# Order of two loops in the score matmuls of a gated scan: blocks outside, heads inside

## The chip, the cores and the metric

The kernel runs on one core of a Trainium2 chip. Its time is that of one execution on the device, in microseconds (us). The engines of the core run side by side and wait for each other through semaphores: TensorE (PE in the profile; its weight loads are PEld), VectorE (DVE), ScalarE (ACT), GpSimd (POOL) and SyncE (SP), which issues DMAs.

## The reference, cut to what matters

The model is one block with a recurrence and dilated attention, then two layers of a hybrid block. In each hybrid layer one branch is a gated linear scan with 4 heads of 64 channels, run forwards (`d` = 0) and backwards (`d` = 1):

```
S_t = diag(f_t) S_{t-1} + k_t v_t^T        o_t = S_t^T q_t
# in chunks; inside a chunk, with a = cumsum(log f):
scores[t, s] = sum_c q[t, c] * k[s, c] * exp(a[t, c] - a[s, c])     for s <= t
out[t] = sum_s scores[t, s] v[s]  +  (q[t] * exp(a[t])) @ state
```

The sum over the 64 channels `c` of one head is the contraction of the score matmuls that this document is about. Sequence: 2048 positions and 256 of context, all in float32.

## The kernel before, in words

`stage_hgrn_scan` (L1339) is called four times: two layers by two directions. It holds the channels on the partitions: a pair `pr` of heads fills 128 partitions, head `h` = 0 on partitions 0 to 63 and head `h` = 1 on 64 to 127. The positions are cut in blocks of 128, and a step of the scan takes `n` blocks: the first step has n = 2 (the context), the four after it n = 4.

The products of gates within a block are built up in levels. A step has LV = 8 levels `lv`, and each level has two parts, one for each pair `pr`. One such part, (lv, pr), is called a group here; a step has 16 of them. In a group

- TensorE computes for each of the two heads and each of the n blocks a 128x128 score matrix over 64 partitions (L1419): stationary operand `kb`, moving operand `qT` at level 0 and `qf` later. The output of head h goes into PSUM bank `pS[pr][h]` (`ps_s` in the profile), one 128-column piece for each block. A float32 matmul shows as two weight loads and two matmuls in the profile, so a group of n = 4 has 16 records of each, one of n = 2 has 8. The last matmul of the group raises `sc`.
- After it TensorE issues one of the eight k-slices of the projection of the next step (L1393, tile `ps_f`, two records over 128 partitions and 512 columns). In the last step of a scan there is no next one, and no such matmul.
- VectorE waits for `sc`, multiplies the gates of this level into `qf` (L1528) and `kb` (L1530), makes the products for the next level (L1532, shorter at each level; it raises `up`), and copies the two banks under the mask of the level into `scores_t` (L1541, twice; at level 0 there is only L1537, twice). The copies raise `cp`.

A group (lv, pr) on TensorE waits for `up` and `cp` of (lv - 1, pr): the operands must be updated, and the banks read. The two pairs take turns, so that VectorE works on one while TensorE works on the other.

After the levels come the transposes of `kb` (L1428), the state matmuls (L1433) and, block by block, the output matmuls (L1445 and L1453, whose operands are 64 columns wide, two heads in turn). VectorE starts the next step with L1512 to L1514, which wait for the last output matmul.

All orders are written out by hand in the loops of each engine; there is no planner. The instructions of TensorE are issued in program order.

Of the kernel before, what the change touches and what calls it, by code (L numbers as in the profile page):

```python
# [13 lines left out]
P = 128  # L14
# [12 lines left out]
HD = 64  # L27
# [1311 lines left out]
def stage_hgrn_scan(env, layer, d, hT, qT, vN, oT, out_ctx):  # L1339
# [17 lines left out]
    with ExitStack() as ctx:  # L1357
# [22 lines left out]
        @block.sync  # L1380
        def _(sp):
            env.load_groups(sp, g + 1 + 1)

        @block.tensor
        def _(pe):
            w = env.group_here(pe, g)

            def project(s, pr, k):
                col, n = steps[s]
                if k == 0 and s >= 1:  # L1390

                    pe.wait_ge(fk.h, fk.at(4 * (s - 1) + 2 * pr + 2))
                mm = pe.matmul(pf[pr][:, 0:n * P], w[:, k, pr * P:(pr + 1) * P], hT[:, k, col:col + n * P],  # L1393
                               start=(k == 0), stop=(k == KT - 1))
                if k == KT - 1:
                    mm.then_inc(pj.h, 1)

            for pr in range(2):
                for k in range(KT):
                    project(0, pr, k)  # L1400
            for s, (col, n) in enumerate(steps):
                for lv in range(LV):
                    for pr in range(2):
                        if lv < 2:
                            pe.wait_ge(qi.h, qi.at(4 * s + 2 * pr + 2))
                        else:
                            pe.wait_ge(up.h, up.at(14 * s + 2 * (lv - 2) + pr + 1))

                        if lv >= 1:
                            pe.wait_ge(cp.h, cp.at(2 * (NU * s + 2 * (lv - 1) + pr) + 2))  # L1410
                        elif s >= 1:
                            pe.wait_ge(su.h, su.at(sum(2 * m for _, m in steps[:s])))
                            pe.wait_ge(tc.h, tc.at(2 * s))
                        for h in range(2):
                            lo = HD * h
                            for i in range(n):
                                cs = slice(i * P, (i + 1) * P)
                                rhs = qT[lo:lo + HD, pr, col + i * P:col + (i + 1) * P] if lv == 0 else qf[lo:lo + HD, pr, cs]
                                mm = pe.matmul(pS[pr][h][:, cs], kb[lo:lo + HD, pr, cs], rhs, start=True, stop=True)  # L1419
                        mm.then_inc(sc.h, 1)  # L1420
                        if s + 1 < NSTEP:
                            project(s + 1, pr, lv)
                for pr in range(2):

                    pe.wait_ge(up.h, up.at(14 * s + 12 + pr + 1))
                    pe.wait_ge(cp.h, cp.at(2 * (NU * s + 2 * (LV - 1) + pr) + 2))
                    for i in range(n):
                        mm = pe.transpose(pS[pr][0][:, i * P:(i + 1) * P], kb[:, pr, i * P:(i + 1) * P], env.ident[:, :])  # L1428
                    mm.then_inc(tm.h, 1)
                for pr in range(2):  # L1430
                    pe.wait_ge(tc.h, tc.at(2 * s + pr + 1))
                    for i in range(n):
                        mm = pe.matmul(pS[pr][1][:, i * P:(i + 1) * P], kbn[:, pr, i * P:(i + 1) * P],  # L1433
                                       vN[:, col // P + i, pr * P:(pr + 1) * P], start=True, stop=True)
                    mm.then_inc(um.h, 1)
                order = range(n - 1, -1, -1) if d else range(n)
                for x, i in enumerate(order):
                    n_done = sum(m for _, m in steps[:s]) + x
                    for pr in range(2):
                        cs = slice(i * P, (i + 1) * P)  # L1440

                        if x == 0 and s >= 1:
                            pe.wait_ge(oc.h, oc.at(2 * (s - 1) + pr + 1))
                        for h in range(2):
                            pe.matmul(pO[pr][HD * h:HD * (h + 1), cs],  # L1445
                                      vN[:, col // P + i, pr * P + h * HD:pr * P + (h + 1) * HD],
                                      sT[:, pr, h, cs], start=True, stop=False)

                        if n_done >= 1:
                            pe.wait_ge(su.h, su.at(2 * (n_done - 1) + pr + 1))  # L1450
                        for h in range(2):
                            lo = slice(HD * h, HD * (h + 1))
                            mm = pe.matmul(pO[pr][lo, cs], st[lo, pr, n_done % 2, lo], qf[lo, pr, cs],  # L1453
                                           start=False, stop=True)
                        mm.then_inc(om.h, 1)
            pe.wait_ge(om.h, om.at(2 * WT))
            pe.sem_inc(env.sem("w_used").h, 1)

        @block.scalar
        def _(act):  # L1460
            def sigmoids(s):
                n = steps[s][1]
                for pr in range(2):
                    act.wait_ge(pj.h, pj.at(2 * s + pr + 1))
                    if s >= 1:

                        act.wait_ge(qi.h, qi.at(4 * (s - 1) + 4))
                    act.activation(fn[:, pr, 0:n * P], pf[pr][:, 0:n * P], ACT.Sigmoid).then_inc(fk.h, 1)
                    act.activation(kn[:, pr, 0:n * P], pf[pr][:, 0:n * P], ACT.Sigmoid, scale=-1.0).then_inc(fk.h, 1)

            sigmoids(0)
            for s, (col, n) in enumerate(steps):
                if s + 1 < NSTEP:
                    sigmoids(s + 1)
                for pr in range(2):
                    act.wait_ge(tm.h, tm.at(2 * s + pr + 1))
                    if s >= 1:
                        act.wait_ge(um.h, um.at(2 * (s - 1) + pr + 1))
                    act.activation(kbn[:, pr, 0:n * P], pS[pr][0][:, 0:n * P], ACT.Copy).then_inc(tc.h, 1)
                if d == 0:  # L1480
                    for pr in range(2):
                        act.wait_ge(om.h, om.at(2 * sum(m for _, m in steps[:s + 1])))
                        act.activation(oT[:, pr, col:col + n * P], pO[pr][:, 0:n * P], ACT.Copy).then_inc(oc.h, 1)
# [13 lines left out]
        def _(dve):  # L1497
# [6 lines left out]
            for s, (col, n) in enumerate(steps):  # L1504
                w = n * P
                ready, done = (fl, 4) if layer == 1 else (fk, 4)
                for pr in range(2):
                    dve.wait_ge(ready.h, ready.at(4 * s + 2 * pr + 2))
                    if s >= 1:
                        dve.wait_ge(tm.h, tm.at(2 * (s - 1) + pr + 1))  # L1510
                        dve.wait_ge(om.h, om.at(2 * sum(m for _, m in steps[:s])))
                    dve.tensor_copy(f[:, pr, 0:w], fn[:, pr, 0:w])  # L1512
                    dve.tensor_copy(kb[:, pr, 0:w], kn[:, pr, 0:w]).then_inc(qi.h, 1)
                    dve.tensor_tensor(qf[:, pr, 0:w], qT[:, pr, col:col + w], fn[:, pr, 0:w], ALU.mult).then_inc(qi.h, 1)  # L1514
# [29 lines left out]
                for x, i in enumerate(order):  # L1544
                    n_done = sum(m for _, m in steps[:s]) + x
                    for pr in range(2):
                        if x == 0:
                            dve.wait_ge(um.h, um.at(2 * s + pr + 1))
                            dve.wait_ge(up.h, up.at(14 * s + 12 + pr + 1))
                        if n_done >= 1:  # L1550

                            dve.wait_ge(om.h, om.at(2 * (n_done - 1) + pr + 1))
                            dve.wait_ge(su.h, su.at(2 * (n_done - 1) + pr + 1))
                        for h in range(2):
                            lo = slice(HD * h, HD * (h + 1))
                            ins = dve.scalar_tensor_tensor(
                                out=st[lo, pr, (n_done + 1) % 2, HD * h:HD * (h + 1)],
                                in0=st[lo, pr, n_done % 2, HD * h:HD * (h + 1)],
                                scalar=pp[lo, pr, poff[7] + i:poff[7] + i + 1],
                                in1=pS[pr][1][lo, i * P + HD * h:i * P + HD * (h + 1)], op0=ALU.mult, op1=ALU.add)  # L1560
                        ins.then_inc(su.h, 1)
# [1110 lines left out]
```

## Time and profile before

| | |
|---|---|
| median of 3 runs | 6555.46 us (6535.63 to 6560.89) |
| span of the profiled execution | 6529.7 us, 77413 instructions |
| the profiled execution's own time | recorded as its span alone |
| mean granted TensorE clock | 0.910 of full speed |
| TensorE matmul, busy | 5885.4 us, 90% |
| TensorE weight loads, busy | 4344.2 us, 67% |
| VectorE, busy | 2844.0 us, 44% |
| ScalarE, busy | 1763.7 us, 27% |

The span runs from the first to the last instruction. Busy is the share of it in which at least one instruction of the engine was under way. The two scans of the first hybrid layer lie between 2116 and 2680 us, those of the second between 4503 and 5040 us. The clock is granted at one of two levels, 0.5 (1.2 GHz) or 1.0 (2.4 GHz).

### The profile page before, as it was taken

Reading aid. Unit: us, or ns where it says so; the run is one execution under the profiler, and the core shown is the slowest. Engines: PE = TensorE matmul, PEld = TensorE weight load, DVE = VectorE, ACT = ScalarE, POOL = GpSimd, SP = SyncE. Lnnn points to the kernel's source line nnn. Section 1 sums busy time; section 2 is a strip of 40 time slices with the busy share of each in tenths; the row PEclk is TensorE's granted clock in tenths of the full one; section 3 lists DMA queues with packets and bytes.
Section 4 is the critical chain, followed back from the end, with each engine's and each line's share of the span. In section 5 each row is a group of like instructions: output and inputs, shape, how many; then the busy total and the mean of one; then the engine's idle time right before and its main releaser. Section 6 shows DMA issues by size and latency. Waiting matters only on the chain. (4 is left out here: it accounts for less than half of the span.)

```text
span 6529.7 us, 77413 instructions
## 1 busy us (share of the span) xinstructions
PE 5885.4 (90%) x30276; PEld 4344.2 (67%) x30276; DVE 2844.0 (44%) x6558; ACT 1763.7 (27%) x4082; POOL 328.0 (5%) x381
## 2 busy tenths in 40 slices
PE   5879998989969999799999988969998899999889
PEld 2338887765548666567777466867666667775667
DVE  2220124433334666625555035345667535551254
ACT  2221015431134000114444123042000134442231
POOL 0000110000010000210000000000000300000000
PEclk8989998857779978799999999989898999999999
DMA  4001110134320000000000111220000000001212
GB/s 158 13 13 50 35 60 28 55 131 136 130 87 20 1 7 1 11 14 1 1 1 1 47 49 49 97 87 14 1 7 1 20 4 1 1 1 33 63 49 94
DMA packets 145404, 256.78 MB, mean 39 GB/s; under 512 B 10796, under 2 KB 89748, under 8 KB 144276
## 3 DMA queue, kind: packets, MB, share of 16 engines
q1 hardware_dynamic: 107700, 211.98, 9.3%
q10 hardware_dynamic: 37344, 39.85, 1.8%
q8 instruction: 244, 4.00, 0.3%
q14 instruction: 116, 0.95, 0.0%
HBM read 195.81 MB, written 55.98 MB: 39 GB/s over the span
## 5 line engine op out<-in xcount | busy, mean ns | idle before, releaser
L1903 PEld LDWEIGHTS ps_pv<-y_t,probs_t 128*128 128x128 f32 x4640 | 588.6, 192 | 153.3 <-issue 142.9
L1980 DVE TENSOR_REDUCE soft<-ps_scores 128x1 f32<-128x512 f32 (+1 forms) x648 | 410.3, 633 | 495.8 <-PE ps_scores L1866 494.7
L1903 PE MATMUL ps_pv<-y_t,probs_t 128*128 128x64 f32 x4640 | 579.7, 270 | 31.4 <-DVE y_t L2018 30.8
L1419 PEld LDWEIGHTS ps_s<-qf,kb 64*128 64x128 f32 x4032 | 423.1, 214 | 194.5 <-DVE products L1532 127.0
L1419 PE MATMUL ps_s<-qf,kb 64*128 64x128 f32 x4032 | 472.8, 315 | 8.6 <-DVE scores_t L1541 8.5
L1277 DVE TENSOR_TENSOR features_low<-h_t,features_high 128x1024 fp32r<-128x1024 f32 x260 | 304.0, 1171 | 354.6 <-ACT features_high L1242 354.1
L644 PE MATMUL ps_proj<-weight_ring,h_t 128*128 128x256 f32 x2048 | 448.5, 381 | 2.7 <-PE ps_proj L644 2.2
L644 PEld LDWEIGHTS ps_proj<-weight_ring,h_t 128*128 128x128 f32 x2048 | 388.9, 191 | 57.6 <-issue 5.4
L1959 ACT ACTIVATE probs<-ps_scores,soft 128x512 f32<-128x512 f32 (+1 forms) x648 | 407.6, 642 | 16.6 <-DVE soft L1989 16.6
L1214 PE MATMUL ps_proj<-features_high,weights_high 128*128 128x512 f32 (+1 forms) x880 | 346.2, 393 | 60.1 <-DVE features_low L1277 30.8
L1945 ACT ACTIVATE probs_t<-ps_pt 128x512 f32<-128x512 f32 (+1 forms) x392 | 205.0, 523 | 686.3 <-PE ps_pt L1883 676.2
L1883 PE MATMUL ps_pt<-ident,probs 128*128 128x128 f32 x2320 | 370.9, 278 | 7.7 <-ACT probs L1959 7.5
L1242 ACT ACTIVATE features_high<-h_t 128x1024 fp32r<-128x1024 f32 x260 | 259.7, 1001 | 420.9 <-PE ps_proj L1214 359.0
L1393 PE MATMUL ps_f<-h_t,weight_ring 128*128 128x512 f32 (+1 forms) x640 | 341.7, 633 | 5.3 <-PEq L1357 2.9
L1541 DVE COPY_PREDICATED scores_t<-level_masks,ps_s 128x512 f32<-128x512 uint8 (+1 forms) x560 | 340.3, 660 | 0.0
L1214 PE MATMUL ps_proj<-features_high,weights_low 128*128 128x512 f32 (+1 forms) x880 | 340.2, 387 | 0.0
L1214 PE MATMUL ps_proj<-features_low,weights_high 128*128 128x512 f32 (+1 forms) x880 | 339.9, 386 | 0.0
L1883 PEld LDWEIGHTS ps_pt<-ident,probs 128*128 128x128 f32 x2320 | 275.3, 150 | 76.3 <-issue 66.4
L1866 PE MATMUL ps_scores<-y_t 128*128 128x512 f32 (+1 forms) x648 | 292.2, 550 | 1.7 <-PEq L1647 1.7
L1866 PE MATMUL ps_scores<-k_second,y_t 128*128 128x512 f32 (+1 forms) x648 | 293.5, 551 | 0.0
L1693 PE MATMUL ps_proj<-weight_ring,h_t 128*128 128x256 f32 x1120 | 256.8, 385 | 27.6 <-PEq L1580 27.6
L1693 PEld LDWEIGHTS ps_proj<-weight_ring,h_t 128*128 128x128 f32 x1120 | 211.5, 193 | 59.1 <-issue 29.8
(308 smaller groups left out, 9159.0 us busy)
## 6 DMA issues: line engine op xcount, KB each, us to landing
weight_ring<-in_w_in_dram SPq DMA_DIRECT2D x40, 1024.0 KB, 6.4
mod_weights<-in_w_mod_dram ACTq DMA_DIRECT2D x24, 1024.0 KB, 5.2
x_rows<-h_rows SPq DMA_DIRECT2D x32, 512.0 KB, 5.9
t_rows<-t_rows SPq DMA_DIRECT2D x64, 256.0 KB, 2.6
x_res<-h_rows SPq DMA_DIRECT2D x32, 512.0 KB, 3.5
res<-result SPq DMA_DIRECT2D x48, 264.0 KB, 2.0
res_rows<-res SPq DMA_DIRECT2D x48, 264.0 KB, 3.9
h_t<-v_rows SPq DMA_DIRECT2D x3, 4096.0 KB, 13.8
```

The source lines that it names most:

```text
L644: mm = pe.matmul(ps[u % 4][:, 0:GC], hT[:, k, t * P:(t + 1) * P], w[:, k, :], start=(k == 0), stop=(k == KT - 1))
L1214: mm = pe.matmul(bank[:, 0:n], w_[:, k0 + k, i * P:(i + 1) * P], f_[:, k, 0:n], start=start, stop=stop)
L1277: dve.tensor_tensor(self.fl[:, s % NB, :, 0:n], self.hT[:, k0:k0 + KS, c0:c0 + n], self.fh[:, s % NB, :, 0:n].bitcast(F32), ALU.subtract). ...
L1393: mm = pe.matmul(pf[pr][:, 0:n * P], w[:, k, pr * P:(pr + 1) * P], hT[:, k, col:col + n * P], start=(k == 0), stop=(k == KT - 1))
L1419: mm = pe.matmul(pS[pr][h][:, cs], kb[lo:lo + HD, pr, cs], rhs, start=True, stop=True)
L1541: dve.copy_predicated(dst, env.levmask[:, 8 * d + l, None, :].to_broadcast([P, n, P]), src)\
L1693: mm = pe.matmul(ps[u % 4][:, 0:GC], hT[:, k, t * P:(t + 1) * P], w[:, k, :], start=(k == 0), stop=(k == KT - 1))
L1866: pe.matmul(ps[c][:, 0:n * P], QT[:, i, t * P:(t + 1) * P], keys[kv][:, (k0 + 4 * c) * P:(k0 + 4 * c + n) * P], start=True, stop=True).the ...
L1883: mm = pe.transpose(pt[c % 2][:, j * P:(j + 1) * P], pr[:, before(u, c) % NPR, j * P:(j + 1) * P], env.ident[:, :])
L1903: mm = pe.matmul(pv[:, 0:HD], pT[:, before(u, c) % 4, j * P:(j + 1) * P], VN[:, k0 + k, kv * HD:(kv + 1) * HD], start=(k == 0), stop=(k == ...
L1959: act.activation(pr[:, i % NPR, 0:n * P], ps[c][:, 0:n * P], ACT.Exp, bias=st[:, b, 0, NC + 1:NC + 2], scale=HD ** -0.5, accum_out=st[:, b ...
L1980: dve.tensor_reduce(st[:, u % 2, 0, c:c + 1], ps[c][:, 0:tiles(u, c) * P], AXX, ALU.max).then_inc(mx.h, 1)
```

## The change

In the group's matmuls the loop over the n blocks becomes the outer one and the loop over the two heads the inner one. The same 2n matmuls are issued with the same operands into the same places of PSUM, and the last one is in both orders that of head 1 and the last block; it raises `sc` as before. No wait, no semaphore, and no other engine's code changes.

```
-                        for h in range(2):
-                            lo = HD * h
-                            for i in range(n):
-                                cs = slice(i * P, (i + 1) * P)
+                        for i in range(n):
+                            cs = slice(i * P, (i + 1) * P)
+                            for h in range(2):
+                                lo = HD * h
                                 rhs = qT[lo:lo + HD, pr, col + i * P:col + (i + 1) * P] if lv == 0 else qf[lo:lo + HD, pr, cs]
                                 mm = pe.matmul(pS[pr][h][:, cs], kb[lo:lo + HD, pr, cs], rhs, start=True, stop=True)
                         mm.then_inc(sc.h, 1)
```

Before, the order for n = 4 is head 0 with blocks 0, 1, 2, 3 and then head 1 with blocks 0, 1, 2, 3. After, it is block 0 with heads 0, 1, then block 1 with heads 0, 1, and so on.

## Rows read from the trace of the kernel before

**Rows 1.** The page: busy time of TensorE, and its granted clock in 40 slices.
```profile
PE 5885.4 (90%) x30276; PEld 4344.2 (67%) x30276; DVE 2844.0 (44%) x6558; ACT 1763.7 (27%) x4082; POOL 328.0 (5%) x381
...
PEclk8989998857779978799999999989898999999999
```

**Rows 2.** Instructions of tile ps_s: count, duration min/median/max in ns, first and last start.
```profile
L1419 PEld LDWEIGHTS ps_s<-qf,kb x4032: 182/188/336, 2119.6 to 5028.2; 64*128 64x128 f32 x192
L1419 PE MATMUL ps_s<-qf,kb x4032: 271/272/580, 2119.6 to 5028.4; 64*128 64x128 f32 x192
L1419 PEld LDWEIGHTS ps_s<-y_t,kb x576: 182/330/335, 2116.2 to 4993.7; 64*128 64x128 f32 x192
...
L1433 PEld LDWEIGHTS ps_s<-y_t,kb_rows x288: 186/192/337, 2145.1 to 5034.8; 128*128 128x128 f32 x144
```

**Rows 3.** Windows over levels of the twelve n = 4 steps with projection: us, busy, clock.
```profile
2150.73:2193.85 43.12, 43.12 (x289) 29.29 (x290) 32.77 (x76) 1.09 (x2) 0.00 (x0) 1.00 0.00 1
...
2425.53:2486.10 60.57, 60.56 (x289) 40.04 (x290) 32.72 (x76) 1.09 (x2) 0.00 (x0) 0.69 0.00 1
...
sum 581.89, PE 581.87 PEld 393.51 DVE 393.14 ACT 13.02 POOL 8.40; mean PE 48.49 PEld 32.79 DVE 32.76 ACT 1.09 POOL 0.70
```

**Rows 4.** Timeline of one group and the next, n = 4, clock 1.0: start, duration.
```profile
2221.66 1.52 PEld L1419 LDWEIGHTS ps_s<-qf,kb 64*128 64x128 f32 x16 [0.76 <-issue]
2221.66 1.71 PE L1419 MATMUL ps_s<-qf,kb 64*128 64x128 f32 x16
...
2223.30 1.12 PE L1393 MATMUL ps_f<-h_t,weight_ring 128*128 128x512 f32 x2
2223.41 0.43 DVE L1528 TENSOR_TENSOR qf<-qf,products 128x256 f32<-128x256 f32 x1 [0.49 <-PE ps_s L1419]
...
2224.29 1.33 DVE L1541 COPY_PREDICATED scores_t<-level_masks,ps_s 128x512 f32<-128x512 uint8 x2
...
2224.36 1.71 PE L1419 MATMUL ps_s<-qf,kb 64*128 64x128 f32 x16
```

**Rows 5.** Timeline of one group of an n = 2 step, clock 1.0.
```profile
2121.35 0.53 PEld L1419 LDWEIGHTS ps_s<-qf,kb 64*128 64x128 f32 x8 [0.76 <-issue]
2121.35 0.72 PE L1419 MATMUL ps_s<-qf,kb 64*128 64x128 f32 x8
2122.00 0.30 PEld L1393 LDWEIGHTS ps_f<-h_t,weight_ring 128*128 128x128 f32 x2
```

**Rows 6.** Timeline of the state matmuls, 128 partitions, clock 1.0.
```profile
2253.04 1.86 PEld L1433 LDWEIGHTS ps_s<-y_t,kb_rows 128*128 128x128 f32 x16
2253.05 2.04 PE L1433 MATMUL ps_s<-y_t,kb_rows 128*128 128x128 f32 x16
```

**Rows 7.** Timeline of the output matmuls, which take the two heads in turn, clock 1.0.
```profile
2255.39 0.44 PE L1453 MATMUL ps_o<-qf,state 64*64 64x128 f32 x4
2255.76 0.20 PEld L1445 LDWEIGHTS ps_o<-scores_t,y_t 128*64 128x64 f32 x4 [0.17 <-issue]
```

**Rows 8.** Timeline of two groups, n = 4, clock 0.5.
```profile
2272.20 3.09 PE L1419 MATMUL ps_s<-qf,kb 64*128 64x128 f32 x16
...
2277.23 3.09 PE L1419 MATMUL ps_s<-qf,kb 64*128 64x128 f32 x16
```

**Rows 9.** Windows over the levels of the four last steps, without projection.
```profile
2327.99:2369.55 41.56, 40.20 (x257) 39.10 (x257) 31.45 (x72) 0.00 (x0) 0.00 (x0) 0.54 0.00 1
...
4713.77:4750.72 36.95, 33.57 (x257) 31.58 (x257) 30.95 (x73) 0.00 (x0) 0.00 (x0) 0.72 0.00 1
...
sum 157.26, PE 148.42 PEld 142.81 DVE 125.20 ACT 0.00 POOL 0.00; mean PE 37.11 PEld 35.70 DVE 31.30 ACT 0.00 POOL 0.00
```

**Rows 10.** Timeline in a last step, clock 1.0.
```profile
2348.80 0.42 DVE L1528 TENSOR_TENSOR qf<-qf,products 128x256 f32<-128x256 f32 x1
...
2349.06 1.68 PE L1419 MATMUL ps_s<-qf,kb 64*128 64x128 f32 x16 [0.35 <-DVE scores_t L1541]
...
2350.82 0.42 DVE L1528 TENSOR_TENSOR qf<-qf,products 128x256 f32<-128x256 f32 x1
```

## The prediction, made before the changed kernel ran

> **What bounds the kernel now.** I began with the page. TensorE is busy 90% of the span and its clock is at full speed for most of it [rows 1], so a shorter stretch of matmuls is worth its time, provided that TensorE is what ends last just there. The instructions of the tile `ps_s` [rows 2] give 4032 + 576 = 4608 matmul records at L1419: 4 scans of one n = 2 step (16 groups of 8) and four n = 4 steps (64 groups of 16).
>
> Then the windows over the levels of each step. There are two kinds of n = 4 step. In twelve steps with the projection beside the scores TensorE is busy 581.87 of 581.89 us, VectorE 32.76 us of 48.49 in the mean [rows 3]: TensorE is the bound. The same rows show the clock: 43.12 us a step at 1.0, up to 60.57 at 0.69. In the four last steps TensorE and VectorE hand over to each other: 157.26 us, of which VectorE is busy 125.20 [rows 9].
>
> The timeline of one group [rows 4] gives the period: 2224.36 - 2221.66 = 2.70 us, of which the scores take 1.64 until the projection starts (2223.30) and the projection 1.06. VectorE has 0.49 us of idle time in a period, waiting for the score matmuls. 16 periods make the 43.12 us.
>
> **What a group's 16 records cost now.** The state matmuls use all 128 partitions, so their loads come one after another: 16 loads in 1.86 us, the last of them 0.19 long, so 15 pitches of (1.86 - 0.19)/15 = 0.111 us [rows 2, 6]. Measure the score groups with that pitch. With n = 4 the 16 loads take 1.52 us: (1.52 - 0.19)/0.111 = 12 pitches, not 15 [rows 4]. With n = 2 the 8 loads take 0.53 us: 3 pitches, where one after another would be 7 [rows 5]. So with n = 2 the two heads, 4 loads each, run wholly side by side, and with n = 4 only 3 of 8 do. My reading: TensorE looks a short way ahead in the program, some 8 instructions (4 pairs of load and matmul). With n = 2, head 0 has 4 pairs, and head 1 is in sight at once. With n = 4, head 0 has 8 pairs, and head 1 comes in sight when the fifth has been issued; it starts 5 pitches late, overlaps for three, and ends alone.
>
> The Trainium skill ("TensorEngine Tiling (Array Packing)", Key Properties) says that different tiles can load weights and multiply in parallel, and that a change of the tiling mode drains the engine. Rows 5 agree with the first, and the second touches nothing here, since both heads use 64x128 tiles.
>
> **The change, part by part.**
> 1. The order. With heads in turn, four pairs of look-ahead always hold both heads: they start together, as with n = 2. The loads then need 7 pitches in place of 12, so a group is shorter by 5. Counted the other way: the n = 2 group takes 0.65 us until the projection starts [rows 5]; four more pairs for each head, side by side, add 4 x 0.111 = 0.44, together 1.10 against 1.64. The saving is 0.54 us a group at clock 1.0, and the period becomes 2.70 - 0.54 = 2.15.
> 2. Whether VectorE lets it. Its work in a step is at most 32.77 us [rows 3]; 16 periods of 2.15 are 34.5. It is covered by 1.7 us a step, and no more: were the score matmuls free, the step could still not fall below about 32. In a period with little product work VectorE's own pitch is 2350.82 - 2348.80 = 2.02 us [rows 10]. The chain of one pair (scores 1.15 to their end, VectorE some 2.2, handing over some 0.2: 3.6) fits into two periods (4.3). So TensorE stays the bound, barely, and the projection and its copies keep their place.
> 3. At clock 0.5 the group takes 3.09 us [rows 8], the period is 2277.23 - 2272.20 = 5.03, and 5 pitches of twice the length save 1.07: 3.96. Both clocks give a period shorter by about a fifth. If the clock rises after the same time as before, the groups that fall into the slow time are more, and a step saves what one at full speed does: 16 x 0.54 = 8.67 us (with the unrounded 0.542). If it rises after as many groups as before, 20% of 581.89 = 116. I take the first: 12 x 8.67 = 104 us.
> 4. The last steps. There is no projection to hide VectorE, and the sum changes kind. Below is VectorE's busy time, 31.3 us a step [rows 9], plus its wait for the first group, 1.2 to 2.1: 32.5 to 33.4. Above is the handing over at clock 0.5: scores 3.09 - 1.07 = 2.0, VectorE 2.1 to 2.2, two signals, 4.4 us a level, 7 of them and a shorter first of 3.5: 34.3. I take 33.5: 157.26 - 4 x 33.5 = 23 us saved. The ends are 130 and 137.2 for the four, so 20 to 27 saved.
> 5. The n = 2 steps: the heads already run side by side [rows 5]. Nothing.
> 6. Everything else (transposes, state, output matmuls, copies, DMAs) keeps its instructions and its waits. A step ends earlier, and so the next starts earlier; the weights for the next stage are loaded during the scan and their landing is far from its end. Nothing.
>
> Sum: 104 + 23 = 127 us. The profiled execution has a span of 6529.7, and would have 6402. The median of the runs is 25.8 us over that span; I carry this over, as something that the change doesn't touch: 6555.5 - 127.4 = **6428 us**.
>
> **The unknown: the clock.** The rows show that a busy TensorE isn't enough to raise it at once: in the step of 2425.53 it was 0.69 in the mean with TensorE busy 60.56 of 60.57 us [rows 3]. All twelve steps together lose 581.9 - 12 x 43.12 = 64 us to the lower clock. If denser matmuls bring it back sooner, up to some 25 us of it are won. If it goes the other way, see the fourth rival.
>
> **Rivals.**
> - *The supply of instructions is the limit.* Side by side, TensorE needs two pairs, 4 instructions, in 0.111 us, 28 ns each. The fastest long stretch that the trace shows is that of the output matmuls, 8 records in 2255.76 - 2255.39 = 0.37 us, 46 ns each [rows 7], though there the change between tile shapes sets the pace. With the first 8 instructions in sight and 24 more at 46 ns, the last starts at 1.10 us, and the group takes 1.31: 0.21 lost of 0.54, 192 groups, 40 us: 6468. For it: no row shows 28 ns over more than the half of a group. Against it: the n = 2 group's 16 instructions come at this rate [rows 5], and 36 instructions in a period of 2.15 are 60 ns in the mean. Chance 0.10.
> - *The change doesn't do what it says*: both orders overlap alike, or the look-ahead isn't what sets head 1 back, but a limit on side-by-side work after a few pairs. Time 6555. Against it is the pair of 3 pitches for 8 loads and 12 for 16. Chance 0.07. The Trainium skill ("TensorE: Matmul & The Clock Gate", the table at its top) gives TensorE a queue of 64 with a partial reorder window. If that window were 64 instructions long, the 32 of a group would fit, head 1 would start with head 0 already today, and the change would be worth nothing. By that rule this rival is the forecast; rows 4, where 16 loads take 12 pitches and not 7, speak against it.
> - *The overlap of today is lost*: with a switch of tile at every matmul the pairs go strictly one after another, 15 pitches in place of 12. A group costs 3 x 0.111 = 0.33 more, 256 groups: 85 us, time 6640. It decides from 12 pitches on. Against it: head by head in turn is what the output matmuls do, and 4 of their records take 0.44 us, 0.27 of it the last matmul's own [rows 2, 7]. Chance 0.04.
> - *The clock falls in the steps with projection*, because TensorE's work is done in less time and VectorE begins to end last; in the last steps, where TensorE has idle time of 0.35 us in a group, the clock is 0.54 to 0.72 [rows 9, 10]. With all twelve steps at 0.5: 12 x 16 x 3.96 = 760 us against 581.9, less 23: 155 us more, 6711. It breaks even where a step with projection takes 50.4 us. Against it: with a period of 2.15 TensorE has no idle time. Chance 0.04.
> - The forecast: 0.75, for the arithmetic rests on two measured groups.
>
> **Range and chances.** The forecast's own range is 6390 to 6455: clock won (25) and runs that differ by 25 us among themselves. For 8 in 10 I add the first rival and leave out the rest: 6385 to 6480. About 0.5%, 33 us, is what a measurement of this kernel can tell from none. Forecast and first rival are faster by more: 0.85. Same 0.07, slower 0.08.
>
> **What the profile of the changed kernel would show.** The n = 4 group: 16 loads in about 0.97 us, 16 matmuls in 1.15, the projection 1.10 after the group's start; the period 2.15 at clock 1.0 and 3.96 at 0.5. VectorE idle before L1528 under 0.1 us in place of 0.49. A step with projection at full clock 34.5 us, a last step 33 to 34. The n = 2 group unchanged at 0.72. I am wrong if the group takes 1.3 us or more, if VectorE's groups take more than 2.15 us in a row so that TensorE waits for `scores_t` in steps with projection, or if the clock in the steps differs.

## The result, and the profile after

| | before | after |
|---|---|---|
| median of 4 runs | 6545.55 us (6517.28 to 6560.89) | 6343.07 us (6334.53 to 6353.71) |
| span of the profiled execution | 6529.7 us | 6351.9 us |
| mean granted TensorE clock | 0.910 | 0.92 |

The ratio is 0.969, with a 95% interval of 0.9662 to 0.9718. The kernel is faster by some 200 us. I had forecast 6428 us and a range from 6385 to 6480: the sign is right, the time is below the range.

The timeline of the changed kernel shows one n = 4 group and what follows, at full clock; the columns are start, duration, engine, line and tile, as in [rows 4]:

```profile
2182.70 0.97 PEld L1419 LDWEIGHTS ps_s<-qf,kb 64*128 64x128 f32 x16 [0.76 <-DVE products L1532]
2182.70 1.16 PE L1419 MATMUL ps_s<-qf,kb 64*128 64x128 f32 x16
2183.80 0.30 PEld L1393 LDWEIGHTS ps_f<-h_t,weight_ring 128*128 128x128 f32 x2
2183.80 1.12 PE L1393 MATMUL ps_f<-h_t,weight_ring 128*128 128x512 f32 x2
2183.91 0.42 DVE L1528 TENSOR_TENSOR qf<-qf,products 128x256 f32<-128x256 f32 x1
...
2184.85 1.16 PE L1419 MATMUL ps_s<-qf,kb 64*128 64x128 f32 x16
```

The 16 loads take 0.97 us in place of 1.52, so 7 pitches of 0.111 us in place of 12. The projection starts 1.10 us after the group, and the period is 2184.85 - 2182.70 = 2.15 us. VectorE's L1528 has no idle time before it, where it had 0.49. All of this is as forecast. What isn't shows in the windows. First the twelve steps with projection (length, busy time and count of PE, PEld, DVE, ACT, POOL, then the clock), to be read against [rows 3]:

```profile
2167.67:2202.03 34.36, 34.36 (x289) 20.52 (x290) 32.30 (x76) 1.08 (x2) 0.00 (x0) 1.00 0.00 1
...
2392.17:2428.11 35.94, 35.94 (x289) 21.25 (x290) 32.30 (x76) 1.08 (x2) 0.00 (x0) 0.95 0.00 1
...
4676.53:4713.81 37.28, 37.28 (x289) 22.49 (x290) 32.27 (x76) 1.09 (x2) 0.85 (x1) 0.91 0.00 1
...
sum 430.81, PE 430.77 PEld 256.55 DVE 387.44 ACT 13.02 POOL 5.12; mean PE 35.90 PEld 21.38 DVE 32.29 ACT 1.09 POOL 0.43
```

At full clock a step takes 34.36 us, and I had 34.5. TensorE is still busy all the time. But the clock is 0.91 or more in every step, where it was down to 0.69. And the four last steps, against [rows 9]:

```profile
2306.03:2338.05 32.02, 22.68 (x257) 19.99 (x257) 30.57 (x72) 0.00 (x0) 0.00 (x0) 0.84 0.00 1
...
4822.71:4854.68 31.97, 21.31 (x257) 18.89 (x257) 30.50 (x73) 0.00 (x0) 0.00 (x0) 0.89 0.00 1
sum 126.95, PE 88.91 PEld 78.13 DVE 122.36 ACT 0.00 POOL 0.00; mean PE 22.23 PEld 19.53 DVE 30.59 ACT 0.00 POOL 0.00
```

VectorE is busy 122.36 of 126.95 us: it is the bound now. TensorE is busy for 70% of the time where it was for 94%, and yet its clock is 0.84 to 0.89 where it was 0.54 to 0.72.

**Where the time came from.** In spans 177.8 us are gone, by stretches:

| stretch | before | after | saved |
|---|---|---|---|
| twelve steps with projection | 581.9 | 430.8 | 151.1 |
| of it, at full clock: 12 x (43.12 - 34.36) | | | 105.1 |
| of it, by a shorter time at the low clock | | | 46.0 |
| four last steps | 157.3 | 127.0 | 30.3 |
| transposes to output matmuls, and the n = 2 steps | | | 5.9 |
| all outside the scans | 5456.5 | 5466.0 | -9.5 |

"Low clock time" below is the time at 0.5 in the twelve windows, 2 x (1 - clock) x length, summed with the unrounded clock; for the window of 60.57 us in [rows 3] it is 2 x 0.31 x 60.57 = 37.6. It was 138.7 us before and is 39.8 after. A scan is counted here from its first score matmul to its last output matmul: 1073.2 us for the four before, 885.9 after. The row of -9.5 is no effect of the change: in a second execution of each kernel (below) the time outside the scans was 5462.6 us before and 5463.4 after. The medians differ by 202.5 us, 25 more than the spans: the profiled execution of before lay below the median of its kernel, that of after (6353.71 us) above its own.

### The profile page after: what moved, and what is told of

Same layout as the page of the kernel before. It is cut to its first block and busy times, and to the rows that moved or that the text cites. A ratio compares the mean times of both kernels' runs of the same rounds, so it can differ in the third digit from the quotient of the medians.

```text
span 6351.9 us, 77413 instructions
## 1 busy us (share of the span) xinstructions
PE 5682.8 (89%) x30276; PEld 4148.8 (65%) x30276; DVE 2833.3 (45%) x6558; ACT 1765.3 (28%) x4082; POOL 328.2 (5%) x381
## 5 line engine op out<-in xcount | busy, mean ns | idle before, releaser
L1419 PEld LDWEIGHTS ps_s<-qf,kb 64*128 64x128 f32 x4032 | 259.8, 195 | 216.0 <-DVE products L1532 118.3
L1419 PE MATMUL ps_s<-qf,kb 64*128 64x128 f32 x4032 | 312.3, 294 | 36.8 <-DVE scores_t L1541 35.8
L1393 PE MATMUL ps_f<-h_t,weight_ring 128*128 128x512 f32 (+1 forms) x640 | 325.8, 607 | 5.3 <-PEq L1357 2.9
```

## The experiments

Two questions: whether the look-ahead works as I had read it, and why the clock came back sooner. Each kernel below is the changed one with the edit shown, except where both kernels run once more, and for the last one, which is the kernel before with an edit.

**Blocks in twos, and three and one.** Two orders between before and after.

```
-for i in range(n):
-    for h in range(2):
+for h, i in [(h, i) for b in range(0, n, 2) for h in range(2) for i in range(b, b + 2)]:           # e3_twos
+for h, i in [(h, i) for b in (range(0, min(n, 3)), range(3, n)) for h in range(2) for i in b]:     # e4_threes
```

> Blocks in twos: head 0 blocks 0, 1; head 1 blocks 0, 1; head 0 blocks 2, 3; head 1 blocks 2, 3. My theory (TensorE looks about 8 instructions, four pairs, ahead): a head has four pairs in a row, as in an n = 2 step before, so the other head is in sight from the start. Group 1.09 to 1.10 us until the projection starts, 16 loads within 0.97 us, time as the changed kernel, 6343 within 0.5%. Rival (it is the turn at every matmul that overlaps, a look-ahead of two pairs): a group of some 1.3 us, 0.2 x 192 = 40 us slower than the changed kernel.

> Blocks three and one: head 0 blocks 0, 1, 2; head 1 blocks 0, 1, 2; head 0 block 3; head 1 block 3. My theory (8 instructions ahead): head 1's first load is the 13th instruction and comes in sight when the fifth has been issued, some two pitches after the start, so the group is 0.2 us longer than the changed one: 1.3 us until the projection, period 2.36, 12 x 16 x 0.21 = 41 us slower than the changed kernel, about 6385. Rival (a look-ahead of three matmuls, 12 instructions, or more): 1.09 us and the time of the changed kernel. Rival (no overlap once a head has more than four pairs): 1.64 us in each group, the time of before or slightly less.

Measured: 6373.88 us (ratio to before 0.9757, interval 0.9719 to 0.9795) and 6439.86 us (0.9854, interval 0.9817 to 0.989). The second is 97 us above the changed kernel, where I had written 41. The weight loads of one group in the timeline of each, first blocks in twos:

```profile
2184.00 1.07 PEld L1420 LDWEIGHTS ps_s<-qf,kb 64*128 64x128 f32 x16 [0.76 <-DVE products L1533]
2185.19 0.30 PEld L1393 LDWEIGHTS ps_f<-h_t,weight_ring 128*128 128x128 f32 x2
```

and three and one:

```profile
2181.08 1.29 PEld L1420 LDWEIGHTS ps_s<-qf,kb 64*128 64x128 f32 x16 [0.76 <-DVE products L1533]
2182.50 0.30 PEld L1393 LDWEIGHTS ps_f<-h_t,weight_ring 128*128 128x128 f32 x2
```

The group takes 1.19 and 1.42 us. In pitches, as (time of 16 loads - 0.19)/0.111: 7.0 for heads in turn, 7.9 for twos, 9.9 for three and one, 12 for head by head. Neither is what I had written (7, and 9), and neither fits the rivals: more head changes aren't what counts, since both orders have three. They do fit a look-ahead of four pairs if it is counted in this way: a pair of load and matmul can be started when the matmul of the pair four places ahead of it in the program has started. The single matmul records of a group start at 0, 0.214 and 0.326 us, so take 0.213 us for the first pair of a run of one head and 0.111 for each after it. With head by head the other head's first pair is the 9th, and waits for the matmul of the 5th, at 0.213 + 3 x 0.111 = 0.55 us: 5 pitches. With three and one it is the 7th and waits for the 3rd, at 0.32: 3 pitches, and here is my slip, for I had taken the fifth instruction in place of the third pair's matmul. With twos the first turn is free, but the second turn of head 1 is the 13th pair and waits for the 9th, which starts its matmul at 0.55 us, about one pitch after head 1 has run out of work. The second turn was missing in my expectation.

The rule was made to fit these times, but the single records of the same groups bear it out. The first load of the other head (told by the two interleaved rows of starts; the records don't name the head) starts at 0.553 us head by head, where the fifth matmul starts at 0.549, and at 0.331 with three and one, where the third starts at 0.327. In twos the load of the 13th pair starts at 0.555 and the matmul of the 9th at 0.550. So the look-ahead is short, four pairs, and of the four orders measured heads in turn, with two pairs of a head in a row, is the best at n = 4.

**Which levels bring the clock back.** Heads in turn at levels 0 and 1 alone, and at levels 2 to 7 alone.

```
+turn = [(h, i) for i in range(n) for h in range(2)]
+head = [(h, i) for h in range(2) for i in range(n)]
+for h, i in (turn if lv < 2 else head):       # e1_first
+for h, i in (head if lv < 2 else turn):       # e2_late
```

> Heads in turn at levels 0 and 1 alone (4 of the 16 groups of a step), head by head at levels 2 to 7. My theory: the changed order gains twice, once through groups that are 0.547 us shorter at full clock, once because denser matmuls at the start of a step bring the clock back sooner. Then here the twelve n = 4 steps with projection have a time at the low clock near that of the changed kernel (39.8 us in all, against 138.7 before), say 35 to 70, and the kernel gains 12 x 4 x 0.547 = 26 us by the groups, some 40 by the clock and some 10 in the last steps: 75 us against before, about 6470. Rival (the lower share of slow clock in the changed kernel is chance, or comes from the shorter step as a whole): low clock time in the twelve steps stays near 110 to 140 us, and the gain is 26 to 40 us: about 6510.

> The complement: head by head at levels 0 and 1, heads in turn at levels 2 to 7 (12 of 16 groups). My theory: at the start of the step, where the clock is low, nothing has changed, so the clock comes back as late as before (low clock time 110 to 140 us in the twelve steps; somewhat less where the low time reached into level 2), and the gain is 12 x 12 x 0.547 = 79 us by the groups and some 20 in the last steps: 100 us, about 6445. Rival (the clock gain is chance or follows the whole step): low clock time near 40 us and a gain of 79 + 40 + 25 = 145 us: about 6400.

Measured: 6455.54 us (0.9877, interval 0.984 to 0.9913) and 6413.3 us (0.9808, interval 0.9765 to 0.9852). Low clock time in the twelve steps: 30.0 us with the first two levels alone, 132.8 without them; I had written 35 to 70 and 110 to 140. The windows of the same view, first for levels 0 and 1 in turn:

```profile
2266.54:2309.08 42.54, 42.54 (x289) 27.96 (x290) 32.65 (x76) 1.09 (x2) 0.00 (x0) 0.96 0.00 1
...
2464.88:2507.39 42.51, 42.51 (x289) 27.81 (x290) 32.67 (x76) 1.09 (x2) 0.00 (x0) 0.96 0.00 1
...
sum 505.06, PE 505.05 PEld 332.50 DVE 391.90 ACT 13.03 POOL 8.41; mean PE 42.09 PEld 27.71 DVE 32.66 ACT 1.09 POOL 0.70
```

and for levels 2 to 7 in turn:

```profile
2428.45:2474.14 45.69, 45.69 (x289) 28.63 (x290) 32.66 (x76) 1.08 (x2) 0.00 (x0) 0.78 0.00 1
...
4821.16:4866.87 45.71, 45.71 (x289) 28.64 (x290) 32.68 (x76) 1.08 (x2) 0.86 (x1) 0.78 0.00 1
sum 500.22, PE 500.21 PEld 312.09 DVE 390.98 ACT 13.02 POOL 5.13; mean PE 41.68 PEld 26.01 DVE 32.58 ACT 1.09 POOL 0.43
```

One fourth of the groups changed gives 76.8 us in the twelve steps, three fourths give 81.7. The first of these numbers can't be had from shorter groups (4 x 12 x 0.547 = 26 us): about 50 us is clock. The medians came out some 15 and 32 us below my numbers. That of the first kernel lies on the side of my theory (6470 against 6510); that of the second lies between the two and nearer to the rival's (6413, with 6445 and 6400 forecast), so it decides nothing. What decides is the low clock time, and the time in the stretches that the theory speaks of: 81.7 and 23.1 us saved in the twelve steps and the last ones, where I had put 79 and 20.

In the step of 45.69 us the clock was low for 19.7 us, about its four head-by-head groups at the low clock (4 x 5.03 = 20.1). It isn't the denser groups that ended this: the clock rose at 2448.13, while the last projection slice before them was under way.

```profile
2446.56 1.89 PE L1393 MATMUL ps_f<-h_t,weight_ring 128*128 128x512 f32 x2
2448.38 1.16 PE L1420 MATMUL ps_s<-qf,kb 64*128 64x128 f32 x16
```

In seven of the eight steps of this kernel in which the clock was low it rose before the first denser group, five times after 19.7 or 19.8 us; in the eighth it rose 4.3 us behind that group's start. What the traces do show is how long it stays low once it has fallen at the start of a step. With head by head in the first levels it is 6.7 to 37.5 us (22 times, in two executions of the kernel before; 3.4 to 23.9 in the kernel with levels 2 to 7 in turn). With heads in turn there it is 3.3 or 3.4 us (16 times, in two executions of the changed kernel) and 6.3 to 6.5 (3 times); it is 3.4 to 6.1 with levels 0 and 1 alone. The orders in between fit: 57.5 us of low clock time in the twelve steps with three and one, 32.7 with twos. Whether the clock is low at all in a given step doesn't follow the order (7 to 11 of the 12 steps, 8 in both kernels of this experiment). The rival, that the step as a whole or chance decides, is out for the length of the low time.

The last steps follow their own order: 149.4 us with levels 2 to 7 head by head, 134.2 with them in turn, 127.0 with all in turn.

**Both kernels once more.**

> The kernel before once more, for a second trace of the clock. My theory: low clock time in the twelve steps with projection is again 100 to 150 us (138.7 in the first trace), because it belongs to the order of the matmuls. Rival (chance of this one execution): it may come out anywhere, also near the 40 us of the changed kernel.

> The changed kernel once more. My theory: low clock time in the twelve steps again 30 to 50 us (39.8 in the first trace), group 1.09 us, time 6343 within 0.3%. Rival (chance): low clock time near 100 us or more, and a span some 25 us longer in the scans.

Low clock time 138.6 us (before, 138.7 the first time) and 33.8 (after, 39.8). The sums of the twelve windows for before and after:

```profile
sum 581.81, PE 581.80 PEld 392.71 DVE 393.31 ACT 13.02 POOL 8.40; mean PE 48.48 PEld 32.73 DVE 32.78 ACT 1.09 POOL 0.70
```

```profile
sum 428.10, PE 428.08 PEld 254.84 DVE 387.50 ACT 13.03 POOL 5.13; mean PE 35.67 PEld 21.24 DVE 32.29 ACT 1.09 POOL 0.43
```

The sum of before is 581.81 us against 581.89 the first time, and 428.10 against 430.81 for after. The sums repeat, while single steps need not: the fourth and fifth step of before were low for 37.5 and 6.8 us the first time, 27.3 and 17.1 the second. The time of after was 6343.93 us (0.9688, interval 0.9655 to 0.972). The single run of before gave 6537.48 us.

**Two projection slices together.** VectorE is busy 32.30 of 34.36 us in a step of the changed kernel, so there should be 2 us to win and no more.

```
                         mm.then_inc(sc.h, 1)
-                        if s + 1 < NSTEP:
-                            project(s + 1, pr, lv)
+                    if s + 1 < NSTEP:
+                        for pr in range(2):
+                            project(s + 1, pr, lv)
```

 Rival (the clock): TensorE's new idle time lets the clock fall as in the last steps, low clock time in the twelve steps rises above 80 us, and the gain is lost: 6345 to 6370. Rival (the change of tile costs nothing): period and time as the changed kernel.

Measured: 6333.47 us (0.9667, interval 0.9633 to 0.9701), 10.5 us below the changed kernel beside it. It is the fastest of all kernels here, though the gain is small beside the spread of the runs (6322.83 to 6336.44, against 6330.96 to 6358.53). Most of it isn't where I had looked. The timeline of two groups:

```profile
2171.17 2.33 PE L1419 MATMUL ps_s<-qf,kb 64*128 64x128 f32 x32
...
2173.44 1.98 PE L1393 MATMUL ps_f<-h_t,weight_ring 128*128 128x512 f32 x4
...
2175.35 0.83 PE L1419 MATMUL ps_s<-qf,kb 64*128 64x128 f32 x10
```

The period of two groups is 4.18 us and not 4.0, against 4.30. Two slices in a row (four records) take 1.91 us, 0.2 less than two by themselves. But the two score groups take 2.27 until the projection, 0.09 more than twice 1.09: a second group of the same tile shape gains nothing. So the two changes of tile shape that are gone saved 0.12 us together, 0.06 each. The 0.2 us that I had put for one is in no run.

At full clock a whole step hardly changed: 34.25 us, where the changed kernel takes 34.36 and I had written 32.5 to 33.

```profile
2157.97:2192.22 34.25, 32.96 (x289) 21.27 (x290) 31.72 (x76) 0.74 (x2) 0.00 (x0) 1.00 0.01 1
```

TensorE is busy for 32.96 of it and idle for 1.29, since the second group now waits for VectorE at some levels (0.86 us once in the first levels). The twelve windows sum to 423.74 us, 7.1 and 4.4 less than in the two executions of the changed kernel; the levels of the four n = 2 steps, where VectorE is far from being the bound, gave 7.2 (104.3 against 111.5 us, from the first score matmul to the first transpose). Low clock time is 32.7 us although TensorE has idle time now, so the rival of the clock didn't come.

**What in the first levels raises the clock.** The kernel before, head by head as it was, with two projection slices behind each group of levels 0 to 3 and none later:

```
                         mm.then_inc(sc.h, 1)
-                        if s + 1 < NSTEP:
-                            project(s + 1, pr, lv)
+                        if s + 1 < NSTEP and lv < LV // 2:
+                            for k in (2 * lv, 2 * lv + 1):
+                                project(s + 1, pr, k)
```

> The kernel before (heads head by head), but with two projection slices behind each group of levels 0 to 3 and none at levels 4 to 7. It asks what in the first levels brings the clock back: in a period at the low clock the array then works on 128 rows for about 3.8 of 6.9 us, in place of 2.0 of 5.0, with the score matmuls side by side no more than before. Theory A (it is how much of the array works in a given time, whichever instructions do it): low clock time in the twelve steps falls from 138.7 to below 80 us. Theory B (it is the side-by-side score matmuls themselves, or the length of a group): it stays at 110 to 150 us. The time as a whole tells nothing here: levels 4 to 7 have nothing that hides VectorE, so the period there is 2.0 to 2.1, and about 3.6 in levels 0 to 3; a step at full clock about 45 us in place of 43.

Measured: 6596.44 us in one run, with 6557.54 for one run of the kernel before beside it. By the measure that I had written down, theory A fell: low clock time in the twelve steps rose to 191.0 us. But the measure mixes two things, and the windows part them. The levels 0 to 3 of three steps in the kernel before:

```profile
2262.53:2295.20 32.67, 32.66 (x145) 21.56 (x145) 15.97 (x36) 0.00 (x0) 0.00 (x0) 0.63 0.00 1
2425.53:2464.54 39.01, 39.01 (x145) 25.28 (x145) 16.79 (x37) 0.00 (x0) 0.00 (x0) 0.52 0.00 1
2498.43:2523.16 24.73, 24.73 (x145) 16.84 (x145) 15.99 (x36) 0.00 (x0) 0.00 (x0) 0.86 0.00 1
```

and of the same three steps with early slices:

```profile
2292.93:2321.35 28.42, 28.42 (x160) 17.57 (x160) 16.82 (x37) 1.09 (x2) 0.00 (x0) 1.00 0.00 1
2450.95:2481.02 30.07, 30.07 (x160) 18.09 (x161) 16.83 (x37) 1.08 (x2) 0.00 (x0) 0.94 0.00 1
2516.05:2546.14 30.09, 30.09 (x160) 17.94 (x160) 16.83 (x37) 1.08 (x2) 0.00 (x0) 0.94 0.00 1
```

In levels 0 to 3 of all twelve steps the low clock time is 37.4 us, against 138.7 before, with not one score matmul more side by side. All the rest, 154 us, lies in levels 4 to 7, where nothing but half-array groups with waits between them is left, and where before had none. So in the first levels either kind of denser work did it: two heads side by side, or more matmuls over all 128 rows between the groups. That the clock follows how much of the array works is my reading of the two together; the split into halves was made after the run, and is not the measure that I had written down before it. Nor does it part the rows at work from other things that changed with them, such as the length of a period or the share of time spent in long matmuls of 512 columns. That the order of the first four groups sets how long the clock stays low is shown; why it does is not.

## Why the prediction was wrong in size

- *The look-ahead and the pitch*: right for this change. 7 pitches, 0.97 us of loads, group 1.10, period 2.15; the twelve steps at full clock saved 105.1 us where I had 104. At the low clock the period of a group in turn is 4.02 us (4529.40 to 4533.42 with levels 2 to 7 in turn) and not 3.96. The look-ahead itself was stated too loosely to carry over: for the two orders in between it missed by one pitch each. The rival of the instruction supply didn't come: a group issues 32 instructions in about 0.9 us, 28 ns each, with no gap.
- *VectorE lets it, barely*: right. TensorE is busy for 430.77 of 430.81 us, VectorE for 387.44.
- *The clock* is the step that failed. I put "12 x 8.67 = 104" on the assumption that the clock rises after the same time as before, set what denser work might win to nothing and bounded it at 25 us. It was 46.0 us in the twelve steps: low clock time fell from 138.7 to 39.8 us. The rows for it were there: a step at 0.69 with TensorE busy throughout [rows 3] says that being busy isn't enough to raise the clock, and I noted it, and went no further. The whole loss of 64 us to the low clock, not a part of it, should have been the bound.
- *The last steps*: 30.3 us and not 23, in the main by the same step. I took 33.5 us, a mean of full and low clock; at a clock of 0.84 to 0.89 it was 31 to 32, on VectorE's busy time. That is also below my lower end of 32.5, which was put together from VectorE's busy time of before (125.20 us in the four, now 122.36) and its wait for the first group.
- *The fourth rival* didn't come: in the twelve steps TensorE has no idle time, as forecast. Its reason had the sign wrong, too. In the last steps TensorE has more idle time than before, with denser work, and the clock is higher, not lower.
- *From span to median*: I carried 25.8 us over from before. The profiled execution after lies 8.8 us above the median of its kernel in its span, so this term was 34.6 us off. This is the spread of single executions and no effect of the change.

The account of the 85.1 us between forecast and median: clock 46.0, last steps 7.0, full clock term 1.1, tails (transposes to output matmuls) and n = 2 steps 5.9, outside the scans -9.5, span to median 34.6. It is reckoned from 104.06 + 23.26 = 127.3 us saved and so from 6428.2, where the prediction's last subtraction has 127.4. With the clock term alone set right the forecast would have been 6382 us, still 39 above the median, of which the step from span to median is 34.6. In the tails the low clock time in the scans but outside the levels went from 19.0 to 9.8 us, so they too gained by the clock; I had put them at nothing.

## What to carry to other kernels

Here, matmuls over 64 rows overlapped with those on the other half of the array only when the other half's instructions were at most about four pairs of load and matmul ahead, and a float32 matmul is two pairs. So put the two halves in turn in the innermost loop, and read the pitch from the trace to see whether they overlap. Where the profile shows a busy TensorE at half clock, try denser work at the start of that stretch: the same edit that made the groups shorter also won back the clock, and here that was worth 46 us beside 105. Bound such a term by all of the time that is lost to the low clock in the stretch.

## What the runs showed that I had not expected

- The clock stayed at 0.5 for 37.5 us while TensorE had no idle time [rows 3], and for 27.3 us in the same step of the second execution (low clock time 138.7 and 138.6 us in the twelve steps).
- Four denser groups at the start of a step brought low clock time from 138.7 to 30.0 us; twelve denser groups after them left it at 132.8.
- The scans before took 1073.2 and 1073.1 us in two executions of 6529.7 and 6535.7 us: the 6 us between these two lie outside them.
